# Expert stage: the 32 remainder slots of each expert transposed as a full 128-partition tile, and their down projection in four column groups

## The chip, the core and the metric

One core of a Trainium2 chip runs the whole program in one launch. The metric is the device time of one execution in microseconds, the median of several runs. The core has a matrix engine (TensorE, PE in the profile; its weight loads stand as PEld), VectorE (DVE), ScalarE (ACT), GpSimd (POOL) and SyncE (SP), which only issues transfers here. Data lie in SBUF, 128 partitions wide; TensorE writes to PSUM, eight banks of 512 float32 values per partition. All data are float32.

## The reference

One inference step of a one-layer encoder for 1024 prompt tokens and 32 sample tokens: a token mixer (sparse attention, gated linear attention and an mLSTM, with a shared input and output projection), a layer norm, and then a mixture of experts, which the change is about:

```python
gate = jnp.einsum('nk,nke->ne', wsel, jax.nn.one_hot(eidx, N_EXPERTS, dtype=F32))
out = jnp.zeros((B * T, D), F32)
for e in range(N_EXPERTS):
    h = jax.nn.silu(xf @ w_gate[e]) * (xf @ w_up[e])
    out = out + gate[:, e:e + 1] * (h @ w_down[e]).astype(F32)
```

There are 16 experts; each token goes to two. D is 1024 and the hidden width 256, so `w_gate[e]` and `w_up[e]` are 1024x256 and `w_down[e]` is 256x1024.

## The kernel before

The program has three stages. The **trunk** computes the mixer tile by tile (nine tiles of up to 128 tokens), the norm and the routing, and writes the normed rows and, for each expert, a list of the tokens that chose it. The **expert stage** (`mlps`) runs the 16 experts one after the other, each over 160 slots (`CAP`): 128 in block 0 and 32 more (`CB`), the remainder, in block 1. `combine` then gathers the two expert rows of each token and does the last norm.

In the expert stage every engine runs its own loop, and semaphores tie them together; each loop holds four experts (`NW`), with buffers by number.

- SyncE loads the three weights of an expert (1 MB each) three experts ahead into one of four sets `wg`, `wu`, `wd`; a set comes free when the down products of its expert are done (`ob_ps`).
- GpSimd loads the slot numbers `ids` and gathers the rows into `xg` (two buffers; block 1 fills partitions 0 to 31 only). A gather waits until the transposes of the expert two before are done. Behind its loop it loads the residual rows `xr` and the gains, and scales nine tiles.
- TensorE, in `body`: 64 instructions for gate and up into `GU` (32 float32 products, each of which runs as two instructions), then `turn` of the next expert, then the down products. `turn` transposes eight 128-column pieces of both blocks into the two halves `T[0]`, `T[1]` of a PSUM pair in turn, two pieces at a time. Down adds up two halves `f` of the hidden width, for block 0 into `OA` (128 rows) and for the remainder into `OB` (32 rows), 512 columns a product.
- ScalarE applies SiLU (`gate`), copies each filled half of `T` to `xgT` (four copies an expert; TensorE may use a half again once its copy is done, `xgT_copied`), copies `OA` to `rows` and issues the stores.
- VectorE multiplies gate and up to `hT` and copies `OB`.

A product of 128 contraction rows whose output has 32 rows uses 32 of TensorE's 128 columns; the profile writes its shape as 128*32. A full one is 128*128, and a transpose of 32 partitions is 32*128. Where the output of a product begins (partition 0, 32, 64 or 96) sets which 32 columns it uses: its column group. In the trunk, line 1397 has products of 64 output rows that begin at partition 0 and 64 in turn:

```python
for h in range(H):
    b = 64 * (h % 2)
    last = mmul(RA[b:b + 64, DV * (h // 2):DV * (h // 2) + DV], qk[0:n, 1, h, :], zvt[:, DV * h:DV * h + DV],
                start=True, stop=True)
```

There are four heads, so four products or eight instructions in a row, all of 96 columns. Line 1142 is the trunk's helper for transposes, line 1666 the gate and up products, 1655 and 1656 the transposes of the two blocks, 1677 the down products.

Of the kernel before, what the change touches and what calls it, by code (L numbers as in the profile page):

```python
# [22 lines left out]
D = 1024  # L23
# [1455 lines left out]
def mlps(nc, a, win, ident, ones, chosen_sum, expert, before, gatew, at_i, more_i, w_at, w_more, xr, g2, b2, ps, x1_d, slot_d, eo_d, em_d):  # L1479
    ctx = ExitStack()  # L1480
    S = semaphores(nc, ctx)
    with ctx:
# [9 lines left out]
        xgT = sb("xgT", [128, 2, KD, CAP])  # L1492
        gate = sb("gate", [128, 2, CAP])
        hT = sb("hT", [128, 2, CAP])
        rows = [sb(f"rows{j}", [128, 2, D]) for j in range(2)]
        most = sb("most", [128, NE])
        in_cap = sb("in_cap", [128, NT, 2])
        pos_f = sb("pos_f", [128, NT, 2])
# [21 lines left out]
        with nc.Block() as block:  # L1520
# [16 lines left out]
            @block.gpsimd  # L1537
            def _(pool):
                pool.sem_inc(S("xgT_ps"), 8)
                with pool.Fori(0, NE // NW) as i:  # L1540
                    for j in range(NW):
                        e = i * NW + j
                        with nc.allow_non_contiguous_dma("slot ids"):
                            pool.dma_start(ids[:, j, 0:1], slots_e[0:128, bass.ds(e, 1), 0]).then_inc(S(f"ids_loaded{j}"), 16)
                            pool.dma_start(ids[0:CB, j, 1:2], slots_e[128:CAP, bass.ds(e, 1), 0]).then_inc(S(f"ids_loaded{j}"), 16)
                        pool.wait_ge(S(f"ids_loaded{j}"), i * 32 + 32)
                        pool.sem_inc(S("pool_passed"), 1)
                        pool.wait_ge(S("xgT_ps"), e * 4 + 4)
                        pool.sem_inc(S("pool_passed"), 1)
                        for b, nb in ((0, 128), (1, CB)):  # L1550
                            pool.indirect_dma_start(  # L1551
                                out=xg[j % 2][0:nb, b, :], out_offset=None, in_=x1_d,
                                in_offset=bass.IndirectOffsetOnAxis(ap=ids[0:nb, j, b:b + 1], axis=0)).then_inc(S(f"xg_loaded{j % 2}"), 16)

                pool.dma_start(xr[:, 0:NPT, :], x1_d[0:SEQ].rearrange("(t p) d -> p t d", p=128)).then_inc(S("xr_loaded"), 16)
                pool.dma_start(xr[0:SMP, NPT, :], x1_d[SEQ:TOKENS]).then_inc(S("xr_loaded"), 16)
                pool.dma_start(g2[:], a["ln2_g"][0].partition_broadcast(128)).then_inc(S("xr_loaded"), 16)
                pool.dma_start(b2[:], a["ln2_b"][0].partition_broadcast(128)).then_inc(S("xr_loaded"), 16)
                pool.wait_ge(S("xr_loaded"), 64)
                for t in range(NT):  # L1560
                    x = xr[0:tokens(t), t, :]
                    nc.gpsimd.tensor_scalar(x, x, ALPHA, None, ALU.mult)

            @block.scalar
            def _(act):
# [6 lines left out]
                def turned(e, j):  # L1572

                    for u in range(4):
                        act.wait_ge(S("xgT_ps"), e * 4 + (u + 9))
                        A.activation(xgT[:, j % 2, 2 * u:2 * u + 2, :], T[u % 2][:, 0:2 * CAP].rearrange("p (k n) -> p k n", k=2),
                                     ACT.Copy).then_inc(S("xgT_copied"), 1)

                def body(i, j, e, last):
# [9 lines left out]
                    act.wait_ge(S("oa_copied"), e + 2)  # L1589
                    act.dma_start(rows_e[0:128, bass.ds(e, 1), :].rearrange("s one d -> s (one d)"), rows[j % 2][:, 0, :]).then_inc(S(f"rows_stored{j % 2}"), 16)  # L1590
                    act.wait_ge(S("ob_copied"), e + 2)
                    act.dma_start(rows_e[128:CAP, bass.ds(e, 1), :].rearrange("s one d -> s (one d)"), rows[j % 2][0:CB, 1, :]).then_inc(S(f"rows_stored{j % 2}"), 16)

                turned(0, 0)

# [7 lines left out]
            def _(dve):  # L1603
# [27 lines left out]
                with dve.Fori(0, NE // NW) as i:  # L1631
                    for j in range(NW):
# [5 lines left out]
                            V.tensor_tensor(hT[:, f, :], gate[:, f, :], GU[f][:, CAP:2 * CAP], ALU.mult).then_inc(S("h_ready"), 1)  # L1638
                        dve.wait_ge(S("ob_ps"), e + (NW + 1))
                        dve.wait_ge(S(f"rows_stored{j % 2}"), i * (16 * NW) + 32 * (j // 2 + 1))  # L1640
                        V.tensor_copy(rows[j % 2][0:CB, 1, :], OB[0:CB, :]).then_inc(S("ob_copied"), 1)  # L1641

            @block.tensor
            def _(pe):
# [4 lines left out]
                def turn(e, j, loaded):  # L1649
                    pe.wait_ge(S(f"xg_loaded{j % 2}"), loaded)  # L1650
                    for u in range(4):
                        pe.wait_ge(S("xgT_copied"), e * 4 + (u + 1))
                        for k in (2 * u, 2 * u + 1):
                            c = CAP * (k % 2)
                            E.transpose(T[u % 2][:, c:c + 128], xg[j % 2][:, 0, 128 * k:128 * k + 128], ident[:])
                            last = E.transpose(T[u % 2][:, c + 128:c + CAP], xg[j % 2][0:CB, 1, 128 * k:128 * k + 128], ident[0:CB, 0:CB])  # L1656
                        last.then_inc(S("xgT_ps"), 1)

                def body(i, j, e, last_one):
# [10 lines left out]
                        turn(e + 1, j + 1, i * (16 * NW) + 32 * ((j + 1) // 2 + 1))  # L1670
                    for f in range(2):
                        pe.wait_ge(S("h_ready"), e * 2 + (f + 3))
                        for out, c0, nb, sem in ((OA, 0, 128, "oa"), (OB, 128, CB, "ob")):
                            if f == 0:
                                pe.wait_ge(S(sem + "_copied"), e + 1)
                            for c in range(2):
                                last = E.matmul(out[0:nb, 512 * c:512 * c + 512], hT[:, f, c0:c0 + nb], wd[j][:, f, 512 * c:512 * c + 512],  # L1677
                                                start=(f == 0), stop=(f == 1))
                            if f == 1:
                                last.then_inc(S(sem + "_ps"), 1)  # L1680

                turn(0, 0, 32)
                each_expert(pe, body)
# [243 lines left out]
```

## Time and profile before

| what | us |
|---|---|
| median of three runs | 1513.97 (1511.3 to 1522.41) |
| span of the profiled execution, first to last instruction | 1520.2 |
| expert stage, first transpose to last product | 1108.8 to 1439.6 of the span |
| TensorE busy in the span | 1318.4 (87%) |
| mean granted TensorE clock over the span | 0.880 of 2.4 GHz |

The span lies within the range of the runs; the program's own time is about the span, a few us of start and end around it. All times of the rows are counted from the start of the span. A row of the order of time gives its start, how long it lasted, the engine, the line and the tiles (output, then inputs) with shapes, and in brackets how long its engine stood idle before it. Durations of single products overlap, since they are pipelined: the distance of two starts is what one costs. The granted clock is 1.00 at 2.4 GHz and 0.50 at 1.2 GHz.

### The profile page before, as it was taken

Reading aid. Unit: us, or ns where it says so; the run is one execution under the profiler, and the core shown is the slowest. Engines: PE = TensorE matmul, PEld = TensorE weight load, DVE = VectorE, ACT = ScalarE, POOL = GpSimd, SP = SyncE. Lnnn points to the kernel's source line nnn. Section 1 sums busy time; section 2 is a strip of 40 time slices with the busy share of each in tenths; the row PEclk is TensorE's granted clock in tenths of the full one; section 3 lists DMA queues with packets and bytes.
Section 4 is the critical chain, followed back from the end, with each engine's and each line's share of the span. In section 5 each row is a group of like instructions: output and inputs, shape, how many; then the busy total and the mean of one; then the engine's idle time right before and its main releaser. Section 6 shows DMA issues by size and latency. Waiting matters only on the chain. (4 is left out here: it accounts for less than half of the span.)

```text
span 1520.2 us, 16147 instructions
## 1 busy us (share of the span) xinstructions
PE 1318.4 (87%) x5597; PEld 813.6 (54%) x5597; DVE 775.7 (51%) x1787; ACT 398.4 (26%) x805; POOL 431.7 (28%) x460
## 2 busy tenths in 40 slices
PE   5898899999999999999898997996289999999800
PEld 2566565755656656656654544653156666666500
DVE  0024125778778878988897988333300000000078
ACT  1142424324324224224314212311011111111111
POOL 5103024052151251261055012002231111113487
PEclk9999899999999898999898988575679999999955
DMA  8966645536543443443333333001078766667163
GB/s 272 313 200 210 231 145 179 173 108 201 155 159 123 146 147 112 146 147 108 113 113 122 110 94 118 1 14 29 4 252 301 235 218 234 211 203 250 35 221 121
DMA packets 146265, 238.60 MB, mean 157 GB/s; under 512 B 17211, under 2 KB 117474, under 8 KB 146194
## 3 DMA queue, kind: packets, MB, share of 16 engines
q1 hardware_dynamic: 131298, 197.66, 40.3%
q0 software_dynamic: 10064, 29.16, 5.9%
q10 hardware_dynamic: 4832, 10.88, 2.3%
q8 instruction: 39, 0.64, 0.2%
q14 instruction: 32, 0.26, 0.1%
HBM read 211.38 MB, written 26.29 MB: 156 GB/s over the span
## 5 line engine op out<-in xcount | busy, mean ns | idle before, releaser
L1188 PE MATMUL bank_pair<-win,xT 128*128 128x384 f32 (+7 forms) x1152 | 450.6, 542 | 14.8 <-DMA win<-in_w_in 13.7
L1188 PEld LDWEIGHTS bank_pair<-win,xT 128*128 128x128 f32 (+1 forms) x1152 | 213.3, 193 | 192.0 <-issue 100.9
L897 DVE MAX8 top<-score 128x8 f32<-128x384 f32 (+6 forms) x201 | 174.9, 870 | 4.0
L898 DVE MATCH_REPLACE8 score<-top,score 128x384 f32<-128x384 f32 (+6 forms) x201 | 171.9, 855 | 0.0
L1282 PE MATMUL bank_pair<-w_out,yT 128*128 128x512 f32 (+1 forms) x288 | 131.2, 610 | 0.4 <-ACT yT L623 0.4
L1641 DVE COPY rows<-bank_pair 32x1024 f32<-32x1024 f32 x16 | 19.4, 1212 | 170.3 <-PE bank_pair L1677 170.3
L567 POOL TENSOR_TENSOR small<-small,pexp 128x4 f32<-128x4 f32 (+1 forms) x9 | 9.4, 1049 | 335.9 <-DVE small L1078 335.9
L1677 PE MATMUL bank_pair<-wd,hT 128*128 128x512 f32 (+1 forms) x192 | 98.8, 653 | 0.0
L1551 POOL DMA_INDIRECT xg<-x_rows,ids x32 | 30.1, 941 | 229.1 <-PE bank_pair L1656 215.9
L1282 PEld LDWEIGHTS bank_pair<-w_out,yT 128*128 128x128 f32 (+1 forms) x288 | 52.8, 186 | 74.0 <-issue 72.2
L1142 PE MATMUL bank_pair<-ident,lm 128*128 128x128 f32 (+2 forms) x234 | 43.2, 312 | 45.8 <-ACT lm L733 15.8
L1638 DVE TENSOR_TENSOR hT<-gate,bank_pair 128x160 f32<-128x160 f32 x32 | 10.3, 321 | 138.6 <-ACT gate L1583 138.6
L918 DVE CUSTOM_DVE_ANT_0 lm<-bank_pair,score 128x128 f32<-128x128 f32 (+8 forms) x36 | 26.0, 723 | 72.9 <-PE bank_pair L1225 50.4
L1142 PEld LDWEIGHTS bank_pair<-ident,lm 128*128 128x128 f32 (+2 forms) x234 | 31.8, 172 | 58.3 <-issue 33.2
L733 ACT ACTIVATE lm<-lm,small 128x128 f32<-128x128 f32 (+8 forms) x36 | 26.9, 748 | 132.0 <-DVE small L920 131.9
L1677 PEld LDWEIGHTS bank_pair<-wd,hT 128*128 128x128 f32 (+1 forms) x192 | 27.0, 160 | 61.5 <-issue 61.0
L1666 PEld LDWEIGHTS bank_pair<-xgT,wg 128*128 128x128 f32 x384 | 53.1, 190 | 10.1 <-issue 10.1
L1666 PE MATMUL bank_pair<-xgT,wg 128*128 128x160 f32 x384 | 57.3, 302 | 0.0
L598 POOL TENSOR_SCALAR rel<-rel,zw 128x512 f32<-128x512 f32 (+4 forms) x33 | 45.2, 1369 | 40.7 <-ACT rel L702 38.6
L1666 PE MATMUL bank_pair<-xgT,wu 128*128 128x160 f32 x384 | 56.1, 299 | 0.0
L1251 PEld LDWEIGHTS bank_pair<-va,pT 128*128 128x128 f32 (+1 forms) x296 | 45.4, 220 | 17.3 <-issue 11.7
L1666 PEld LDWEIGHTS bank_pair<-xgT,wu 128*128 128x128 f32 x384 | 53.5, 190 | 0.0
(339 smaller groups left out, 2091.7 us busy)
## 6 DMA issues: line engine op xcount, KB each, us to landing
win<-in_w_in SPq DMA_DIRECT2D x90, 768.0 KB, 4.4
win<-in_w_in SPq DMA_DIRECT2D x18, 1024.0 KB, 5.3
win<-in_w_in SPq DMA_DIRECT2D x18, 840.0 KB, 5.2
win<-in_w_in SPq DMA_DIRECT2D x18, 800.0 KB, 4.6
wg<-in_w_exp_gate SPq DMA_DIRECT2D x12, 1024.0 KB, 6.2
wu<-in_w_exp_up SPq DMA_DIRECT2D x12, 1024.0 KB, 9.4
wd<-in_w_exp_down SPq DMA_DIRECT2D x12, 1024.0 KB, 11.1
expert_rows<-rows ACTq DMA_DIRECT2D x16, 512.0 KB, 3.3
```

The lines of the kernel that those rows point to most:

```text
L598: ins = G.tensor_scalar(r if h else sc, r, zw[0:n, t % 2, h:h + 1], None, ALU.mult)
L733: A.activation(lm[0:n, 0:K], lm[0:n, 0:K], ACT.Exp, bias=sm(n, ANEG + h), scale=HA ** -0.5, accum_out=sm(n, ASUM + h)).then_inc(S("probs_r ...
L897: step(V.max(top8[0:n], sc))
L898: step(V.match_replace(sc, top8[0:n], sc, NEG))
L918: step(V.tensor_tensor_reduce(lm[0:n, 0:K], SC[0:n, 0:K], score[0:n, t % 2, 0:K], 1.0, -3.0e38, ALU.add, ALU.max, sm(n, AMAX + h)))
L1142: tr = lambda out, in_: E.transpose(out, in_, ident[0:in_.shape[0], 0:in_.shape[0]])
L1188: last = mmul(zb[0:n, 0:w], xT[:, kk, 0:n], win[:, i % NWIN, k, 0:w], start=(kk == 0), stop=(kk == KD - 1))
L1251: last = mmul(MA[0:n, HA * h:HA * h + HA], pT[0:kb, g % 2, b - b0, 0:n], vv[:, HA * h:HA * h + HA], start=(b == 0), stop=(128 * b + kb == K))
L1282: last = mmul(SC[0:n, 512 * c:512 * c + 512], yT[:, k, 0:n], w_out[:, k, 512 * c:512 * c + 512], start=(k == 0), stop=(k == KD - 1))
L1551: pool.indirect_dma_start(out=xg[j % 2][0:nb, b, :], out_offset=None, in_=x1_d, in_offset=bass.IndirectOffsetOnAxis(ap=ids[0:nb, j, b:b + ...
L1666: last = E.matmul(GU[f][:, CAP * m:CAP * m + CAP], w[:, k, 128 * f:128 * f + 128], xgT[:, j % 2, k, :], start=(k == 0), stop=(k == KD - 1))
L1677: last = E.matmul(out[0:nb, 512 * c:512 * c + 512], hT[:, f, c0:c0 + nb], wd[j][:, f, 512 * c:512 * c + 512], start=(f == 0), stop=(f == 1))
```

## The change

The remainder is treated in a new shape in two places, and its result lies in another form.

- **Transposes.** Block 1 is transposed over all 128 partitions, like block 0, so all 16 transposes of an expert have one shape. Partitions 32 to 127 of block 1, which no gather writes, are cleared once by GpSimd before its loop, in both `xg` buffers. A half of `T` now holds four pieces of 128 columns; ScalarE copies the first 160 of each 256.
- **Down products.** Block 0 comes first as a whole, both halves `f`. Then the remainder: eight products of 256 columns, four for each `f`, whose outputs go to partitions 0, 32, 64 and 96 of the same 256 columns of `OB`: quarter `q` of the model width into column group `q`. `OB` is then 128 partitions by 256.
- **Copy and store.** VectorE copies 128x256 into a new tile `rest`; ScalarE stores it with a pattern that puts the quarters back in place.

```diff
-        rows = [sb(f"rows{j}", [128, 2, D]) for j in range(2)]
+        rows = [sb(f"rows{j}", [128, 1, D]) for j in range(2)]
+        rest = [sb(f"rest{j}", [128, D // 4]) for j in range(2)]
...
                 pool.sem_inc(S("xgT_ps"), 8)
+                for x in xg:
+                    nc.gpsimd.memset(x[:, 1, :], 0.0).then_inc(S("rest_cleared"), 1)
+                pool.wait_ge(S("rest_cleared"), 2)
                 with pool.Fori(0, NE // NW) as i:
...
-                        A.activation(xgT[:, j % 2, 2 * u:2 * u + 2, :], T[u % 2][:, 0:2 * CAP].rearrange("p (k n) -> p k n", k=2),
+                        A.activation(xgT[:, j % 2, 2 * u:2 * u + 2, :], T[u % 2].rearrange("p (k n) -> p k n", k=2)[:, :, 0:CAP],
                                      ACT.Copy).then_inc(S("xgT_copied"), 1)
...
-                    act.dma_start(rows_e[128:CAP, bass.ds(e, 1), :].rearrange("s one d -> s (one d)"), rows[j % 2][0:CB, 1, :]).then_inc(S(f"rows_stored{j % 2}"), 16)
+                    act.dma_start(rows_e[128:CAP, bass.ds(e, 1), :].rearrange("s one (q d) -> q s (one d)", q=4), rest[j % 2][:]).then_inc(S(f"rows_stored{j % 2}"), 16)
...
-                        V.tensor_copy(rows[j % 2][0:CB, 1, :], OB[0:CB, :]).then_inc(S("ob_copied"), 1)
+                        V.tensor_copy(rest[j % 2][:], OB[:, 0:256]).then_inc(S("ob_copied"), 1)
...
                         for k in (2 * u, 2 * u + 1):
-                            c = CAP * (k % 2)
-                            E.transpose(T[u % 2][:, c:c + 128], xg[j % 2][:, 0, 128 * k:128 * k + 128], ident[:])
-                            last = E.transpose(T[u % 2][:, c + 128:c + CAP], xg[j % 2][0:CB, 1, 128 * k:128 * k + 128], ident[0:CB, 0:CB])
+                            for b in range(2):
+                                c = 256 * (k % 2) + 128 * b
+                                last = E.transpose(T[u % 2][:, c:c + 128], xg[j % 2][:, b, 128 * k:128 * k + 128], ident[:])
                         last.then_inc(S("xgT_ps"), 1)
...
                         pe.wait_ge(S("h_ready"), e * 2 + (f + 3))
-                        for out, c0, nb, sem in ((OA, 0, 128, "oa"), (OB, 128, CB, "ob")):
-                            if f == 0:
-                                pe.wait_ge(S(sem + "_copied"), e + 1)
-                            for c in range(2):
-                                last = E.matmul(out[0:nb, 512 * c:512 * c + 512], hT[:, f, c0:c0 + nb], wd[j][:, f, 512 * c:512 * c + 512],
-                                                start=(f == 0), stop=(f == 1))
-                            if f == 1:
-                                last.then_inc(S(sem + "_ps"), 1)
+                        if f == 0:
+                            pe.wait_ge(S("oa_copied"), e + 1)
+                        for c in range(2):
+                            last = E.matmul(OA[:, 512 * c:512 * c + 512], hT[:, f, 0:128], wd[j][:, f, 512 * c:512 * c + 512],
+                                            start=(f == 0), stop=(f == 1))
+                    last.then_inc(S("oa_ps"), 1)
+                    pe.wait_ge(S("ob_copied"), e + 1)
+                    for f in range(2):
+                        for q in range(4):
+                            last = E.matmul(OB[CB * q:CB * q + CB, 0:256], hT[:, f, 128:CAP], wd[j][:, f, 256 * q:256 * q + 256],
+                                            start=(f == 0), stop=(f == 1))
+                    last.then_inc(S("ob_ps"), 1)
```

How TensorE's instructions stand, from the first quarter of the transposes of one expert to the down products of the one before it. The rows give the line, the operation, output and inputs, and the output's shape; one down product stands for two instructions on the chip. Before, the end of the transposes and the down products:

```order
L1652 REGISTER_ALU
L1655 MATMUL bank_pair<-ident,xg 128x128
L1656 MATMUL bank_pair<-ident,xg 128x32
L1655 MATMUL bank_pair<-ident,xg 128x128
L1656 MATMUL bank_pair<-ident,xg 128x32
L1672 REGISTER_ALU
L1677 MATMUL bank_pair<-win,hT 128x512 x2
L1677 MATMUL bank_pair<-win,hT 32x512 x2
L1672 REGISTER_ALU
L1677 MATMUL bank_pair<-win,hT 128x512 x2
L1677 MATMUL bank_pair<-win,hT 32x512 x2
```

And after, the same place:

```order
L1656 REGISTER_ALU
L1660 MATMUL bank_pair<-ident,xg 128x128 x4
L1676 REGISTER_ALU
L1680 MATMUL bank_pair<-win,hT 128x512 x2
L1676 REGISTER_ALU
L1680 MATMUL bank_pair<-win,hT 128x512 x2
L1686 MATMUL bank_pair<-win,hT 32x256 x8
```

The two shapes of transpose no longer take turns, and the 32-row products stand in one run of eight behind all of the 128-row ones.

On GpSimd, where the expert stage begins, before:

```order
L1537 UNCONDITIONAL_BRANCH
L1540 UNCONDITIONAL_BRANCH
L1540 ISA
L1544 DMA ids<-slot_tokens 128x1
L1545 ISA
L1545 DMA ids<-slot_tokens 32x1
```

And after:

```order
L1538 UNCONDITIONAL_BRANCH
L1542 MEMSET xg 128x1024 x2
L1544 UNCONDITIONAL_BRANCH
L1544 ISA
L1548 DMA ids<-slot_tokens 128x1
L1549 ISA
L1549 DMA ids<-slot_tokens 32x1
```

Two clears now stand ahead of the first load of slot numbers, and of every gather behind it.

## Rows read from the trace of the kernel before

**Rows 1.** The page, busy time, share of the span and instructions of TensorE

```profile
PE 1318.4 (87%) x5597; PEld 813.6 (54%) x5597; DVE 775.7 (51%) x1787; ACT 398.4 (26%) x805; POOL 431.7 (28%) x460
```

**Rows 2.** Windows: start:end, us, busy us by engine (instructions), granted clock, DMA share, GB/s

```profile
1108.80:1439.60 330.80, 330.05 (x1536) 212.19 (x1536) 28.54 (x48) 57.89 (x115) 71.44 (x71) 0.95 0.65 219
...
1165.00:1185.00 20.00, 20.00 (x89) 12.18 (x88) 1.85 (x3) 3.38 (x7) 3.01 (x4) 0.91 0.63 209
1185.00:1205.00 20.00, 20.00 (x101) 13.21 (x100) 1.85 (x3) 4.66 (x8) 3.04 (x4) 1.00 0.69 233
```

**Rows 3.** Groups by form, expert stage: busy us, mean ns of one, idle before

```profile
L1677 PE MATMUL bank_pair<-wd,hT 128*32 128x512 f32 x96 | 45.9, 600 | 0.0
```

**Rows 4.** Order of time, TensorE, three experts: their gate and up products

```profile
1198.21 8.96 PE L1666 MATMUL bank_pair<-xgT,win 128*128 128x160 f32 x64
...
1219.50 2.44 PE L1666 MATMUL bank_pair<-xgT,wg 128*128 128x160 f32 x16
...
1239.20 0.40 PE L1666 MATMUL bank_pair<-xgT,wg 128*128 128x160 f32 x1
```

**Rows 5.** Order of time, TensorE, transposes of one expert, then its down products

```profile
1228.30 0.27 PE L1655 MATMUL bank_pair<-ident,xg 128*128 128x128 f32 x1
1228.50 0.24 PE L1656 MATMUL bank_pair<-ident,xg 32*128 32x32 f32 x1
1228.67 0.33 PE L1655 MATMUL bank_pair<-ident,xg 128*128 128x128 f32 x1
...
1229.11 0.33 PE L1655 MATMUL bank_pair<-ident,xg 128*128 128x128 f32 x1
...
1231.70 0.70 PE L1677 MATMUL bank_pair<-wd,hT 128*128 128x512 f32 x1
```

**Rows 6.** Order of time, TensorE in the trunk: eight full transposes

```profile
628.31 1.04 PE L1142 MATMUL bank_pair<-ident,y 128*128 128x128 f32 x8
```

**Rows 7.** Order of time, first expert: last copy of the transposes, then products

```profile
1114.07 0.44 ACT L1576 ACTIVATE xgT<-bank_pair 128x320 f32<-128x320 f32 x1 [0.86 <-PE bank_pair L1656]
...
1114.64 10.51 PE L1666 MATMUL bank_pair<-xgT,win 128*128 128x160 f32 x64 [0.61 <-ACT xgT L1576]
```

**Rows 8.** Order of time, weight loads of down products in the expert of rows 5

```profile
1234.50 0.11 PEld L1677 LDWEIGHTS bank_pair<-wd,hT 128*32 128x32 f32 x1 [0.32 <-issue]
1235.45 0.30 PEld L1677 LDWEIGHTS bank_pair<-wd,hT 128*128 128x128 f32 x2 [0.84 <-issue]
1235.99 0.19 PEld L1677 LDWEIGHTS bank_pair<-wd,hT 128*128 128x128 f32 x1 [0.24 <-issue]
1236.42 0.19 PEld L1677 LDWEIGHTS bank_pair<-wd,hT 128*128 128x128 f32 x1 [0.24 <-issue]
```

**Rows 9.** Order of time, line 1397: all of it, and what had begun by 616.98

```profile
616.97 0.55 PE L1397 MATMUL bank_pair<-zv,qk 128*64 128x96 f32 x8
...
616.97 0.30 PE L1397 MATMUL bank_pair<-zv,qk 128*64 128x96 f32 x2
```

**Rows 10.** Windows: a stretch of transposes, what followed it, and one in the trunk

```profile
1206.60:1210.01 3.41, 3.41 (x20) 2.21 (x18) 0.32 (x1) 1.53 (x4) 0.00 (x0) 1.00 0.83 320
1210.01:1213.42 3.41, 3.41 (x7) 1.51 (x6) 0.00 (x0) 0.52 (x2) 1.62 (x2) 0.50 0.15 17
936.90:1008.60 71.70, 61.68 (x255) 43.22 (x256) 28.86 (x110) 25.03 (x50) 7.30 (x12) 0.50 0.08 26
```

**Rows 11.** Order of time, GpSimd: the largest clear in the trunk

```profile
17.80 0.73 POOL L488 MEMSET zm<- 128x776 f32 x1
```

**Rows 12.** Order of time, VectorE in the expert of rows 5

```profile
1219.71 1.21 DVE L1641 COPY rows<-bank_pair 32x1024 f32<-32x1024 f32 x1 [11.77 <-PE bank_pair L1677]
...
1228.91 0.32 DVE L1638 TENSOR_TENSOR hT<-gate,bank_pair 128x160 f32<-128x160 f32 x1 [4.02 <-ACT gate L1583]
```

**Rows 13.** Order of time, GpSimd behind its last gather

```profile
1375.51 1.00 POOL L1551 DMA_INDIRECT xg<-x_rows,ids  x1 [18.07 <-PE bank_pair L1656]
...
1398.08 24.67 POOL L1562 TENSOR_SCALAR xr<-xr 128x1024 f32<-128x1024 f32 x9 [17.77 <-DMA b<-in_ln_b]
```

## The prediction

> **What bounds the kernel now.** I read the page's engine totals first, then the expert stage by windows, its groups by form, and its order of time. On the page TensorE is busy for 87% of the span and no other engine for more than 51% [rows 1]. In the expert stage (330.8 us from the first transpose to the last product) it is busy for 330.05 us, with a mean granted clock of 0.95 and the DMA engines at a share of 0.65 [rows 2]. What TensorE is spared here therefore comes off the span, as long as nothing else becomes late. The groups by form show that the down products that make only 32 output rows are as many as those that make 128 and last 0.60 us each [rows 3]. The order of time gives one expert: gate and up start at 1219.50, transposes at 1228.30, down products at 1231.70, the next expert at 1239.20, so 8.80 + 3.40 + 7.50 = 19.70 us [rows 4, 5].
>
> **Transposes.** Now a 128-partition transpose is followed by a 32-partition one; a pair takes 0.43 us (1228.67 to 1229.11), eight pairs 3.40 us [rows 5]. Yet eight full transposes in a row take 1.04 us, the last itself 0.27, so 0.11 us from one to the next [rows 6]: the changes of shape cost, not the columns. Sixteen full ones need 15 x 0.11 + 0.11 = 1.75 us if nothing waits. But ScalarE empties two buffers in turn, at 0.44 us a copy [rows 7], and a quarter of the work is now four transposes, 0.44 us too. Step by step: the fourth transpose ends at 0.60, the first copy at 1.07; TensorE follows a copy 0.13 us later (copy end 1114.51, product start 1114.64 [rows 7]), so the third quarter starts at 1.20. The second copy ends at 1.53, the last quarter runs from 1.66 to 2.10. I take 2.1 us, a saving of 1.3 an expert, 19.7 us for 15. The bounds are 1.75 us (no wait, 25 saved) and today's 3.40 (nothing). The first expert's transposes run at half clock, 5.8 us from 1108.8 to 1114.64 [rows 2, 7]; at twice 0.11 us each, with the closing copy, some 4.3: 1.5 us saved.
>
> **Down products.** A float32 product is two instructions. The weight loads tell the steps at 512 columns: 0.43 us (1235.99 to 1236.42), alike in both shapes. From 1234.50 to 1235.45 are two steps and the return from 32 to 128 columns, 0.09 us for the change; the next step, to 1235.99, is 0.54, so 0.11 more [rows 8]. An expert has four changes, 7.50 - 16 x 0.43 = 0.6 us in all, 0.15 each. After it there are two, and the 128-row part is eight steps, 3.43 us. The remainder becomes 16 instructions of 256 columns, 0.21 us each. What they take hangs on whether four groups of 32 columns run at once. The trace has two groups of 64 at once: the products of line 1397 alternate between output partitions 0 and 64, and their eight instructions of 96 columns are over in 0.55 us, one lasts up to 0.30, and two have begun within the first 0.02 us [rows 9]. Four pairs then begin (0.55 - 0.30) / 3 = 0.08 us apart, which is what 96 columns cost one alone (0.43 x 96 / 512). Today's 32-row products all lie in one column group, and their two halves follow each other at 0.43 us; so the two that start together belong to different heads. I take full overlap: four steps of 0.21 and 0.2 us for what of the changes falls to this part, 1.06. Down is then 4.5 us and saves 3.0, 48 us over 16 experts. With no overlap it is 3.43 + 0.2 + 3.43 = 7.06 us, a saving of 0.44, or 7. The other end is worse still: if each of the eight changes of group also cost 0.2 us, the dearest change of shape here, down would take 8.66 us and lose 1.16 an expert, 19 in all. The nearest row is that of line 1397, with the same data type and column groups in turn.
>
> The Trainium skill, page "TensorE: Matmul & The Clock Gate", section "Part 3: Packing small matmuls", says that matmuls start and end strictly in program order; by that rule the first of the rivals below would hold, 17 us above the forecast. The two starts of line 1397 [rows 9] disagree with it. The same section's measured gain of 2.38 times with three column groups agrees with overlap as such, and no run here shows three or four.
>
> **The clock.** It falls to 0.50 right behind a stretch of transposes: 1.00 from 1206.60 to 1210.01, which are nearly all transposes, then 0.50 until 1213.42 [rows 10]. That expert took 1219.50 - 1198.21 = 21.29 us, 1.59 more than its neighbour [rows 4]. The windows of 20 us from 1125 to 1405 show seven such dips (one in the second of [rows 2], 0.91 against 1.00), together 11.1 us. All seven follow some 3.4 us of transposes; eight stretches of the same length are followed by none. After the change a stretch has 2.1, so I count the dips as gone (the bounds: 0 and 11.1; if they stay, 1450). The Trainium skill, same page, section "Part 4: PE-mode transpose", says that transposes do not count as busy for the clock in the way that products do. The dips agree; by that rule any stretch of transposes is a risk, and sixteen full ones still make one.
>
> **Start, end and queues.** GpSimd clears two 128x1024 tiles and waits for that before it loads the first slot numbers; the first gather is queued behind it, and TensorE waits for the gather. A clear of 776 columns took 0.73 us [rows 11]; so 2 x 0.97 and a wait, 2.0 us lost. The last copy, 32x1024 in 1.21 us [rows 12], becomes 128x256; a VectorE operation on 160 columns of PSUM took 0.32 [rows 12], so about 0.4: 0.8 saved. The remainder's store goes to 128 partitions of 1 KB; ScalarE's queue has room and the buffer is used again two experts later, so nothing. The wait for the remainder's last copy now stands behind the 128-row products, and that copy is done more than 10 us before [rows 8, 12]. The wait for the second half of the hidden rows moves ahead of two products: those rows are ready at 1229.23, 2.5 us before the products begin [rows 4, 12], and after the change still over 1 us before.
>
> **Who is late next.** Weights, gathers and stores: the DMA share is 0.69 in undisturbed windows of 20 us [rows 2], so 13.6 us of work an expert against the coming 15.4. That is 0.88, and loads run three experts ahead: hidden, with 1.8 us to spare. GpSimd: from the last gather at 1375.51 it loads the residual rows (waits 17.8 us) and scales nine tiles until 1422.75 [rows 13], 47.2 us. TensorE has left at that point the down products of expert 12, two whole experts and one without transposes: 4.5 + 2 x 15.4 + 8.8 + 4.5 = 48.6, less 0.9 that had passed since the transposes. GpSimd stays hidden by 0.5 us and the last copy and store behind TensorE; a slower load would soon show.
>
> **Sum.** 19.7 + 1.5 + 48 + 11.1 + 0.8 - 2.0 = 79 us. Against the profiled execution (span 1520.2; the slowest run, 1522.41, is 2.2 above it) this gives 1443; against the median of 1513.97 it gives 1435. The quicker runs may already lack some dips, so I take 1439.
>
> **The rivals.** *Overlap in program order:* in the program the two halves of a product stand side by side; if starts keep that order, only the second half of one group's product overlaps the first half of the next group's. That is nine steps of 0.21 us in place of four, 1.07 us an expert, 17 us: 1456. For it speaks that all other products here do run in order. *The groups don't overlap:* the change would not do what it says; 2.56 us an expert, 41 us: 1480, and with a price at each change of group (1.6 us more) 1506. *The end or the DMA takes over:* the scaling by GpSimd ends last, or weights come late, 3 to 10 us: about 1445. *The clock stays down, and the kernel gets slower:* a busy engine alone does not hold it, since from 936.9 to 1008.6 TensorE was busy for 61.68 of 71.70 us at 0.50 [rows 10], with small shapes and transposes. The stage after has 4.3 + 10.4 + 15 x 10.9 + 16 x 4.5 = 250 us of TensorE's work; the gain of 79 us is used up when the mean granted clock of the stage falls to 250 / 329 = 0.76, and below that the time is over 1518, for instance 1540. Against it: 12.2 of 15.4 us are the same full-array products that hold 1.00 now.
>
> **How the numbers follow.** Forecast 0.60; program order 0.15; no overlap 0.10; end or DMA 0.10; clock 0.03; the rest anything. The range from 1423 to 1463 takes in the forecast, the lost clock dips, the end and the program-order case, and leaves out no overlap and the clock. A measurement of this kernel tells about 1% from no change; all cases but the clock's lie more than 1% (15 us) below 1514, some ends of the second and third excepted: faster 0.95, same 0.02, slower 0.03.
>
> **What would show it.** In the profile after: 16 transposes 0.11 us apart with two short waits for ScalarE; the remainder's 16 instructions over in about 1.1 us, four begun almost at once; an expert of 15.4 us; no dip in the clock between 1130 and the stage's end; two clears of about 1 us ahead of the first slot numbers. I am wrong if the remainder takes 1.9 us or more, if GpSimd or a weight load releases TensorE, or if the dips stay.

## The result, and the profile after

The changed kernel took 1444.08 us (median of four runs, 1429.1 to 1448.7), the kernel before, on the same chip, 1517.43 (four runs): a ratio of 0.951, 95% interval 0.944 to 0.9585. It is faster by 73 us. The forecast was 1439. Timed once more later (e10 below) it took 1441.12 against 1518.40, 77 us less.

The profiled execution is the quickest of the four, 1429.1 us with a span of 1427.3. On the page TensorE is as busy by share as before [rows 1], with less work:

```profile
PE 1226.1 (86%) x5725; PEld 791.4 (55%) x5725; DVE 760.8 (53%) x1787; ACT 398.6 (28%) x805; POOL 433.6 (30%) x462
```

The windows of the stage, in the columns of [rows 2]: the whole stage, a window near its start, the two windows of [rows 2], and the window of [rows 10] in which the clock had been down.

```profile
1096.80:1346.00 249.20, 246.54 (x1664) 197.59 (x1664) 16.66 (x47) 58.01 (x115) 70.96 (x71) 0.99 0.85 290
1105.00:1125.00 20.00, 19.33 (x136) 16.23 (x135) 1.39 (x4) 4.97 (x9) 5.42 (x8) 1.00 1.06 357
1165.00:1185.00 20.00, 19.91 (x140) 16.87 (x139) 1.39 (x4) 4.97 (x9) 3.03 (x4) 1.00 1.03 343
1185.00:1205.00 20.00, 19.82 (x141) 16.53 (x140) 1.39 (x4) 4.89 (x11) 3.03 (x4) 1.00 1.01 344
...
1210.01:1213.42 3.41, 3.41 (x27) 3.41 (x27) 0.09 (x1) 0.00 (x0) 0.00 (x0) 1.00 0.66 228
```

The stage is 249.1 us long (1096.85 to 1345.93) where it was 330.7. Its clock is 1.00 behind the first transposes, and no window shows a dip. The DMA share is 0.85 on average, but 1.01 to 1.06 in the three windows up to 1205, where before it was 0.63 and 0.69. The share adds up the times of the packets, and these can overlap, so it can pass 1. The order of time of TensorE in one expert and of ScalarE beside it, the answer to [rows 4, 5, 7]:

```profile
1209.45 2.44 PE L1670 MATMUL bank_pair<-xgT,wg 128*128 128x160 f32 x16
...
1218.24 2.22 PE L1660 MATMUL bank_pair<-ident,xg 128*128 128x128 f32 x16
1220.30 3.60 PE L1680 MATMUL bank_pair<-wd,hT 128*128 128x512 f32 x8
1223.83 1.07 PE L1686 MATMUL bank_pair<-wd,hT 128*32 128x256 f32 x16
1224.83 3.39 PE L1670 MATMUL bank_pair<-xgT,win 128*128 128x160 f32 x23
```

```profile
1218.88 0.88 ACT L1580 ACTIVATE xgT<-bank_pair 128x320 f32<-128x320 f32 x2
1220.06 0.88 ACT L1580 ACTIVATE xgT<-bank_pair 128x320 f32<-128x320 f32 x2 [0.31 <-PE bank_pair L1660]
```

Start to start, an expert is 8.79 of gate and up, 2.06 of transposes, 3.53 of 128-row products and 1.00 of the remainder: 15.38 us, where it was 19.70. How the remainder begins shows in two windows of the same view: up to 0.07 us behind its first start (first row) four instructions have begun, up to 0.37 us (second row) eight.

```profile
1223.83 0.42 PE L1686 MATMUL bank_pair<-wd,hT 128*32 128x256 f32 x4
1223.83 0.64 PE L1686 MATMUL bank_pair<-wd,hT 128*32 128x256 f32 x8
```

The waits of TensorE in the stage (us in total, times, longest):

```profile
PE bank_pair L1660 <- issue: 11.0, 1, 11.0
PE bank_pair L1670 <- ACT xgT L1580: 0.6, 1, 0.6
PE bank_pair L1670 <- DMA wd<-in_w_exp_down: 0.6, 1, 0.6
```

The first lies ahead of the stage, the second is that of [rows 7]. The third is new: the second expert waits 0.6 us for its weights. GpSimd ahead of the first gather, the answer to [rows 11]:

```profile
1085.32 1.84 POOL L1542 MEMSET xg<- 128x1024 f32 x2 [6.22 <-POOLq L104]
1088.30 0.60 POOL L1548 DMA_DIRECT2D ids<-slot_tokens  x1 [1.14 <-issue]
...
1091.81 1.02 POOL L1555 DMA_INDIRECT xg<-x_rows,ids  x1 [2.33 <-issue]
```

The same in the kernel before:

```profile
1099.87 0.60 POOL L1544 DMA_DIRECT2D ids<-slot_tokens  x1 [6.98 <-POOLq L104]
...
1103.68 1.02 POOL L1551 DMA_INDIRECT xg<-x_rows,ids  x1 [2.32 <-issue]
```

From the end of the trunk's last GpSimd work to the first gather it is now 6.22 + 6.49 = 12.71 us; before it was 6.98 + 3.81 = 10.79. The clears cost 1.9 us.

The end has got longer. From the last product to the first gather of the combine stage it is 9.63 us (1345.93 to 1355.56), before 6.68 (1439.47 to 1446.16). The last products and the first gathers, after and then before:

```profile
1344.86 1.07 PE L1686 MATMUL bank_pair<-wd,hT 128*32 128x256 f32 x16
...
1355.56 1.05 POOL L1843 DMA_INDIRECT r<-expert_rows,at_i  x1 [8.85 <-PEq L1812]
```

```profile
1432.01 7.46 PE L1677 MATMUL bank_pair<-wd,hT 128*128 128x512 f32 x16
...
1446.16 1.04 POOL L1835 DMA_INDIRECT r<-expert_rows,at_i  x1 [23.40 <-PEq L1804]
```

GpSimd's scaling [rows 13] and the last store on ScalarE's queue, in order of time, and then by line 1521, the end of the block, at which all engines meet (duration in ns, first and last start; the end of an engine's DRAIN row is taken as its arrival):

```profile
1322.02 24.69 POOL L1566 TENSOR_SCALAR xr<-xr 128x1024 f32<-128x1024 f32 x9 [19.01 <-DMA b<-in_ln_b]
```

```profile
1346.46 0.55 ACTq L1596 DMA_DIRECT2D expert_rows<-rest  x1
```

```profile
L1521 POOLq EVENT_SEMAPHORE  x2: 17/17/17, 1352.4 to 1352.5; - x2
L1521 POOLq DRAIN  x1: 30365/30365/30365, 1322.0 to 1322.0; - x1
...
L1521 ACTq DRAIN  x1: 8/8/8, 1351.5 to 1351.5; - x1
```

And the kernel before, where this is line 1520:

```profile
L1520 POOLq DRAIN  x1: 30345/30345/30345, 1398.0 to 1398.0; - x1
...
L1520 ACTq DRAIN  x1: 8/8/8, 1442.9 to 1442.9; - x1
```

Two things are seen. ScalarE, which waits for the last store, arrives at 1351.5, 5.6 us after the last product (before: 1442.9, 3.5 us). And GpSimd's drain, which begins with the scaling, lasts 30.37 us, until 1352.3, which is 5.6 us behind the end of the scaling's row (1346.71); so GpSimd is the last to arrive, by 0.8 us. In the kernel before the drain of 30.35 us lasts until 1428.4, long before the last product. What GpSimd does in these 5.6 us the rows don't show. They aren't the price of longer scalings: the drain ends 5.63 us behind the last row in all twelve profiled executions, with nine scalings and, in e8 and e9 below, with seven.

What the store does shows in the busy share of the DMA engines in 40 equal slices of 1346.8 to 1351.4:

```profile
DMA  6999979699973520206010032222222221000000
```

The 512 KB of the 128-row store fill all 16 engines for 1.4 us. The remainder's 128 KB go on until 1351.0; for the last 1.4 us the share is 0.2, about three to four engines of 16. In the kernel before, from 1439.3 to 1442.8, the remainder's store is the second block, 0.6 us long:

```profile
DMA  0009899997979997970000000099669510000000
```

The same two views also count the packets, after first and then before; the third row is e7's (below, 1367.3 to 1371.0), in which the remainder is stored as four:

```profile
DMA packets 276, 0.66 MB, mean 142 GB/s; under 512 B 20, under 2 KB 148, under 8 KB 276
DMA packets 192, 0.66 MB, mean 187 GB/s; under 512 B 32, under 2 KB 32, under 8 KB 192
DMA packets 336, 0.66 MB, mean 177 GB/s; under 512 B 80, under 2 KB 208, under 8 KB 336
```

Those under 512 B are packets of 4 bytes, which carry none of the rows. With two stores in the kernel before there are 32, with five in e7 80, so 16 for a store that uses all engines. In the kernel after there are 20: 16 for the 128-row store and 4 for the remainder's. That agrees with four engines, by a count and not by a share.

Accounting, profiled against profiled: the stage -81.6 us, its start +1.9, its end +2.9, together -76.8. The medians differ by 73 and 77. The rest of the 93 us between the two spans isn't the change's: the unchanged trunk ended 14 us earlier in this execution, and the combine stage took 71.7 us for 74.0 (73.4 when profiled again in e10).

### The profile page after: what moved, and what is told of

Same layout as the page of the kernel before. It is cut to its first block and busy times, and to the rows that moved or that the text cites. A ratio compares the mean times of both kernels' runs of the same rounds, so it can differ in the third digit from the quotient of the medians.

```text
span 1427.3 us, 16405 instructions
## 1 busy us (share of the span) xinstructions
PE 1226.1 (86%) x5725; PEld 791.4 (55%) x5725; DVE 760.8 (53%) x1787; ACT 398.6 (28%) x805; POOL 433.6 (30%) x462
## 5 line engine op out<-in xcount | busy, mean ns | idle before, releaser
L1645 DVE COPY rest<-bank_pair 128x256 f32<-128x256 f32 x16 | 6.8, 425 | 91.6 <-PE bank_pair L1686 91.6
L530 POOL DMA_INDIRECT slot_tokens<-tok_id,slots_i x18 | 18.5, 1029 | 115.0 <-DVE chosen_sum L997 95.0
L1251 PE MATMUL bank_pair<-va,pT 128*128 128x64 f32 (+1 forms) x296 | 47.5, 304 | 0.4 <-ACT pT L623 0.4
```

The lines of the kernel that those rows point to most:

```text
L1251: last = mmul(MA[0:n, HA * h:HA * h + HA], pT[0:kb, g % 2, b - b0, 0:n], vv[:, HA * h:HA * h + HA], start=(b == 0), stop=(128 * b + kb == K))
```

## The experiments

The theory on record: the remainder's gain comes from four column groups at work at the same time; that of the transposes from full shapes in a row, which also takes the clock's dips away. Rivals: groups overlap only as far as program order lets them; the gain comes from something else in the rewrite (the shorter copy, the order of the products); the dips come from the 32-row products or from the length of a stretch of transposes. The measured numbers below are the stage from first transpose to last product, and the parts of an expert start to start.

**e1 and e2: each part alone.** e1 has the transposes, their copies and the clears of the changed kernel, and the down products, the remainder's copy and the stores of the one before; e2 the reverse. Excerpts, against the kernel after:

```
# e1
-  E.matmul(OB[CB * q:CB * q + CB, 0:256], hT[:, f, 128:CAP], wd[j][:, f, 256 * q:256 * q + 256], ...)
+  E.matmul(out[0:nb, 512 * c:512 * c + 512], hT[:, f, c0:c0 + nb], wd[j][:, f, 512 * c:512 * c + 512], ...)
# e2
-  last = E.transpose(T[u % 2][:, c:c + 128], xg[j % 2][:, b, 128 * k:128 * k + 128], ident[:])
+  E.transpose(T[u % 2][:, c:c + 128], xg[j % 2][:, 0, 128 * k:128 * k + 128], ident[:])
+  last = E.transpose(T[u % 2][:, c + 128:c + CAP], xg[j % 2][0:CB, 1, 128 * k:128 * k + 128], ident[0:CB, 0:CB])
```

> Full transposes and the clears as in the changed kernel, down products, copy and store as before. If the changes of shape are what transposes cost and long stretches of transposes are what drops the clock: transposes 2.06 us an expert, down 7.40, an expert 18.26 us, no dip in the clock, TensorE's stage from the first transpose to the last product 294 us (before 330.6, changed 249.1), time 33 to 36 us below the kernel before, and 6.7 us from the last product to the first gather of the next stage, as before. Rival, the 32-row products are what drops the clock: about seven dips stay, stage 305 us.

> Four column groups with the new copy and store, transposes in the old two shapes, no clears. First theory: transposes 3.4 us, down 4.6, an expert 16.85 us, dips of the clock behind about half of the stretches of transposes, stage 273 us and 1.6 us more for each dip, time 42 to 52 us below the kernel before; 9.6 us from the last product to the first gather, because the store of 128 pieces of 1 KB lands late. Rival on the clock (32-row products one after the other drop it): no dip. Rival on the end (GpSimd's scaling holds it up): 6.7 us there, since this stage is longer and GpSimd done long before.

e1: 1480.81 us against 1517.88, ratio 0.974 (0.967 to 0.980). Stage 296.4 us, transposes 2.06, down 7.39, no dip, end 6.68. e2: 1464.39, ratio 0.9665 (0.962 to 0.971). Stage 278.2, transposes 3.41, down 4.6, and the end at 8.82, although GpSimd's drain was over 4.6 us before ScalarE arrived: so the longer end begins with the store. Of the dips of the clock three were left, behind stretches of 3.41 us with alternating shapes; one of them by its window:

```profile
1234.40:1237.80 3.40, 3.40 (x6) 1.69 (x6) 0.00 (x0) 0.44 (x1) 1.88 (x2) 0.50 0.25 58
```

What follows: both parts work alone, and the products of 32 rows don't bring the dips, since e1 has them all and no dip.

**e3 and e4: group by group, and one group.** e3 writes the remainder's products in another order, all of one group and then all of the next; e4 keeps e3's order and its 16 instructions of 256 columns, but puts all their results into column group 0, with the copy and the store of the kernel before. Excerpts:

```
# e3, against after
-  for f in range(2):
-      for q in range(4):
+  for q in range(4):
+      for f in range(2):
# e4, against e3
-  E.matmul(OB[CB * q:CB * q + CB, 0:256], ...)
+  E.matmul(OB[0:CB, 256 * q:256 * q + 256], ...)
```

> As the changed kernel, but the remainder's products in the order of the groups, both halves of the hidden width of a group next to each other, so four instructions of one group follow each other in the program. If each column group takes its own instructions in turn, whatever stands between them: the remainder 1.0 us, as in the changed kernel, stage 249 us. If starts keep the program's order: only a group's last step overlaps the next one's first, 13 steps, 2.7 us, stage 276 us.

> As the changed kernel, with the same eight products of 256 columns for the remainder, group by group, but all into output partitions 0 to 31, so in one column group; copy and store as before. If the gain is overlap between groups: 16 steps of 0.21 us, the remainder 3.6 us, an expert 18.0, stage 291 us. If the gain came from fewer changes of shape and from the order alone: the remainder stays near 1 us, stage 250 us.

One run each. e3: 1440.86 us (before 1517.88), stage 249.3, remainder 1.02. e4: 1473.58, stage 289.5, remainder 3.57. The 16 instructions of one expert, e3 first:

```profile
1218.96 1.09 PE L1686 MATMUL bank_pair<-wd,hT 128*32 128x256 f32 x16
```

```profile
1230.16 3.64 PE L1685 MATMUL bank_pair<-wd,hT 128*32 128x256 f32 x16
```

In e3 four instructions have again begun within 0.08 us of the first, and eight within 0.33 (first two rows); in e4 one has begun within 0.09 us (third row).

```profile
1234.37 0.44 PE L1686 MATMUL bank_pair<-wd,hT 128*32 128x256 f32 x4
1234.37 0.66 PE L1686 MATMUL bank_pair<-wd,hT 128*32 128x256 f32 x8
```

```profile
1230.16 0.40 PE L1685 MATMUL bank_pair<-wd,hT 128*32 128x256 f32 x1
```

What follows: the same instructions cost 3.57 us in one group and 1.02 in four (1.00 in the kernel after), so the gain is overlap. And it doesn't hang on the order in the program: in e3 the first four instructions written all go to group 0, which in e4 takes one each 0.22 us. Four that begin within 0.08 us must then belong to four groups, so that later instructions of other groups overtake earlier ones. The records don't name the group; this is read from the total and from the spacing, and the spacing bears it out: the four starts lie 7 ns apart in the kernel after and 13 ns in e3, twice as much, and the first instructions of two groups lie two apart in the one program and four in the other.

**e5 and e6: what the shapes cost, and what lowers the clock.** e5 is the kernel before with the four transposes of a quarter in the order 128, 128, 32, 32 partitions; e6 is the kernel after with all transposes of a quarter done twice. Excerpts:

```
# e5, against before
+  for k in (2 * u, 2 * u + 1):
       E.transpose(T[u % 2][:, c:c + 128], xg[j % 2][:, 0, ...], ident[:])
+  for k in (2 * u, 2 * u + 1):
       last = E.transpose(T[u % 2][:, c + 128:c + CAP], xg[j % 2][0:CB, 1, ...], ident[0:CB, 0:CB])
# e6, against after
-  for k in (2 * u, 2 * u + 1):
+  for k in (2 * u, 2 * u + 1) * 2:
```

> The kernel before, with the four transposes of a quarter in the order 128, 128, 32, 32 partitions instead of 128, 32, 128, 32. Theory (each change of shape costs TensorE about 0.1 us, the work of a 32-partition transpose no more than that of a full one): eight changes fewer in each expert, 3.40 us of transposes become about 2.6, the stage 330.7 - 15 x 0.8 = 319 us or less. Rival (a 32-partition transpose itself takes 0.3 us): the transposes stay at 3.4 us, whatever the order. On the clock: if a stretch of transposes as long as 3.4 us lets it drop, the seven dips go with the shorter stretch; if the 32-partition form does, they stay.

> The kernel after, with every full transpose done twice, so that a stretch of transposes is as long as before the change without having a 32-partition one: 32 x 0.109 = 3.5 us for 2.06, the period 15.39 + 1.4 = 16.8 us, the stage 249 + 15 x 1.4 = 270 us. Theory (the length of the stretch between matmuls lets the clock drop): dips come back in a part of the experts, 3 to 8 of 15. Rival (the small form or its gaps do it): none. ScalarE's copies are faster than the doubled quarters, so that TensorE should wait for none of them.

One run each. e5: 1491.9 us (before 1521.68), transposes 2.37 for 3.41, stage 302.9, no dip. e6: 1462.14 us, transposes 3.49, stage 271.8, no dip. A quarter of e5, and the clock of both stages behind their first transposes (e5's window first):

```profile
1236.61 0.44 PE L1655 MATMUL bank_pair<-ident,xg 128*128 128x128 f32 x2
1236.97 0.31 PE L1658 MATMUL bank_pair<-ident,xg 32*128 32x32 f32 x2
1237.21 0.44 PE L1655 MATMUL bank_pair<-ident,xg 128*128 128x128 f32 x2
```

```profile
1120.00:1410.00 290.00, 290.00 (x1485) 191.92 (x1484) 28.47 (x47) 55.52 (x111) 65.48 (x63) 1.00 0.72 243
```

```profile
1110.00:1375.00 265.00, 264.39 (x1882) 221.52 (x1881) 16.67 (x47) 56.11 (x112) 68.74 (x68) 1.00 0.79 272
```

What follows: eight changes of shape fewer save 1.04 us, 0.13 each on average, with the same work; the rival that a small transpose is itself dear falls. Start to start in e5, a small one behind a small one takes 0.084 us, less than the 0.109 of a full one in e9 below; a step into the other shape takes 0.20 or 0.15. So the kernel before could have had 28 us of its stage by a change of order alone (15.6 us of transposes, the rest mainly the dips). On the clock the theory that a stretch of transposes need only be long gets no support: in one execution each, 3.49 us of full ones in e6 lowered it in none of 15 experts, 3.41 us of alternating ones in seven (before) and in three (e2). What decides in which of them is open.

**e7: the remainder's store as four.** The store has the four groups as its outermost dimension. e7 issues one store for each group instead (an excerpt, against the kernel after).

```
-  act.dma_start(rows_e[128:CAP, ...].rearrange("s one (q d) -> q s (one d)", q=4), rest[j % 2][:])
+  for q in range(4):
+      act.dma_start(rows_e[128:CAP, ..., 256 * q:256 * q + 256], rest[j % 2][CB * q:CB * q + CB, :])
```

> The kernel after, with the remainder's store issued as four stores of 32 partitions instead of one whose outermost dimension is the four groups. Theory (one store with an outermost dimension of four is spread over four DMA engines only, 32 pieces of 1 KB one behind the other on each): the last store has landed about 3.5 us after TensorE's last product, against 5.4 us; the combine stage starts hardly earlier, since GpSimd, whose scaling then arrives last, holds it at 8.4 to 9.6 us after the last product. Rival (128 pieces of 1 KB take that long however they are spread): 5.3 us as now. If the four loaded engines also delay the weights, the wait of 0.6 us at expert 1 gets shorter.

e7 took 1452.64 us in its one run (before 1521.68). ScalarE arrived 4.1 us after the last product (1370.5 against 1366.45) where it had been 5.6, though the four issues alone took 2.15 us. But the first gather came 10.93 us after it, later than in the kernel after, since GpSimd arrived at 1374.2:

```profile
L1521 POOLq DRAIN  x1: 30348/30348/30348, 1343.8 to 1343.8; - x1
...
L1521 ACTq DRAIN  x1: 8/8/8, 1370.5 to 1370.5; - x1
```

The store part of the theory holds; the expected 8.4 to 9.6 us was too low, GpSimd arriving 3.6 us behind ScalarE here and not 0.8. The second expert's wait for weights was longer (2.3 us), so the four loaded engines aren't what it comes from.

**e8, e9 and e10: what can be mended.** e8 takes e7's stores, clears the tiles on VectorE, lets VectorE scale the last two of the nine tiles, and has VectorE copy the odd quarters of the transposes. e9 is e8 with all copies on ScalarE again, but a third buffer for the transposes: the remainder now fills only one of the two banks that it used to, and the other is free. e10 is the kernel after, unchanged, timed beside e9.

```
# e9, excerpts against after (stores as in e7)
-  nc.gpsimd.memset(x[:, 1, :], 0.0)
+  V.memset(x[:, 1, :], 0.0)
-  T = [ps[1][:, 0:512], ps[1][:, 512:1024]]
+  T = [ps[1][:, 0:512], ps[1][:, 512:1024], ps[3][:, 512:1024]]
-  pe.wait_ge(S("xgT_copied"), e * 4 + (u + 1))
+  if u in (0, 3):
+      pe.wait_ge(S("xgT_copied"), e * 4 + (2 if u == 0 else 3))
-  for t in range(NT):
+  for t in range(NT - 2):
+  for t in range(NT - 2, NT):
+      V.tensor_scalar(x, x, ALPHA, None, ALU.mult)
```

> The kernel after with four things mended: the two clears on VectorE instead of GpSimd, the remainder's store as four stores, the last two tiles of the end's scaling on VectorE, and the copies of the odd quarters of transposes on VectorE, those of the even ones on ScalarE. Expected: the stage's start 2 us earlier, 2.06 -> 1.75 us of transposes (15 x 0.31 = 4.6 us), 9.6 -> 6.8 us between the last product and the first gather of the combine stage; in all 9 us less than after, 1435 us, a ratio of 0.945 to before. Rival (the weights are the bound of the first experts, and the DMA engines are busy 0.85 of the stage): the transposes' gain turns into waits for weights, and the time is 1439 us.

> The kernel after with the two clears on VectorE, the remainder's store as four stores, the last two tiles of the end's scaling on VectorE, and a third buffer for the transposes in the half of the fourth bank pair that the remainder's products no longer use; ScalarE makes all copies. In the two-engine variant the transposes stayed at 2.11 us, since both engines' copies begin only 0.3 us after a quarter's last transpose and so the third quarter still waited for its buffer. Theory (the wait is for the buffer): 16 x 0.109 = 1.75 us of transposes for 2.06, no wait among them; with the start 2.5 us earlier and 2.6 us less at the end some 9 us less than after. Rival (the copies themselves are the bound, and the down products then wait): transposes 2.06 us or the same sum with the next phase.

> The kernel after, unchanged, timed on the same chip as the variant with the third buffer. Expected: 0.952 of before as in its first runs (0.944 to 0.9585), some 9 us over the variant. If the weights' arrival at the second expert depends on when the trunk ends, its wait differs from the 0.6 us of the first profile, between nothing and 2.4 us.

e8: 1435.76 us, ratio 0.944 (0.940 to 0.948). Its end came out as expected (7.05 us), its transposes did not: 2.11 us, since the first copy ends no earlier than before, so that the third quarter waits as it did, and VectorE's copy (0.49 us to ScalarE's 0.44) then holds the fourth by another 0.06 us. e9: 1430.74 us, ratio 0.942 (0.937 to 0.947), against 0.950 (0.946 to 0.9545) of e10, 1441.12 us. It is 10.4 us less than the kernel after on the same chip, where 9 had been expected; the intervals touch, but five of e9's six runs are quicker than the quickest of e10's. The profile shows where it comes from: in e9 the transposes are done in 1.75 us without a wait, and GpSimd is no longer the last to arrive.

```profile
1229.47 1.91 PE L1667 MATMUL bank_pair<-ident,xg 128*128 128x128 f32 x16
1231.22 3.60 PE L1687 MATMUL bank_pair<-wd,hT 128*128 128x512 f32 x8
```

```profile
L1521 POOLq DRAIN  x1: 24885/24885/24885, 1332.1 to 1332.1; - x1
...
L1521 ACTq DRAIN  x1: 8/8/8, 1358.7 to 1358.7; - x1
```

Its end is 7.27 us (e10: 10.12), its stage 246.2 (e10: 249.7), and the clears no longer stand ahead of the first gather (10.80 us behind the trunk's last GpSimd work, against 12.72 in e10). So this is the quickest of the versions here, 5.8% below the kernel before. The second expert's data came late in both: in e9 TensorE waited 2.43 us for it ahead of the transposes, in e10 for its weights behind them:

```profile
1124.12 2.44 PE L1670 MATMUL bank_pair<-xgT,wg 128*128 128x160 f32 x16 [1.24 <-DMA wd<-in_w_exp_down]
```

## Why the prediction was right

The forecast of 1439 us lies 5 us under the first median and 2 under the second. The sum of 79 us stands against 76.8 by the profiles; that the forecast was put in the middle between 1443 and 1435, since quicker runs may lack some dips, no run bears out or refutes. Its mechanism, overlap of four groups and full shapes in a row, is the one the runs show. By its terms:

- *Transposes, 3.40 to 2.1, 19.7 us.* Measured 3.41 to 2.06 in all 15, 20.2 us. One wait for ScalarE, not two: the first copy ends at 1.07 us as reckoned, TensorE follows it 0.05 us later and not 0.13, and the second copy ends at 1.51, so the fourth quarter's buffer is free by the time the third is through. The bound of 1.75 is what e9 reaches with a third buffer.
- *First expert, 5.8 to 4.3.* Measured 5.82 to 4.26.
- *Down, 7.50 to 4.5, 48 us.* Measured 7.50 to 4.53, 47.4 us. The 128-row part takes 3.53 and the remainder 1.00, where 3.43 and 1.06 stood; probably one change of shape lies in the other part.
- *Clock, 11.1 us.* Summing what the seven dips added to the parts of their experts gives 11.4 us, and all are gone. The reason was half right: that they follow 3.4 us of transposes is true of every one, but in e6 the length alone did nothing. The risk that the prediction still saw in sixteen full ones showed in none of the 15 stretches of the kernel after.
- *Last copy, 0.8.* 1.21 to 0.42. But the store behind it took up more than this (below).
- *Clears, -2.0.* Measured -1.9, given back in e9.
- *DMA share 0.88.* Measured 0.85 over the stage, so the weights stay hidden on the whole; but the share is about 1 until about 1205, and the second expert waits 0.6 us (1.2 and 2.3 in other executions). By the prediction's own mark, "if GpSimd or a weight load releases TensorE", it was wrong here, and again at the end (below); in the stage this is partly set off, since the kernel before lost 1.55 us in its first expert, between gate and up and the next transposes, and this one nothing. Such a wait for the second expert's data stood in every execution but two, sometimes before its transposes and sometimes behind; what decides its length was not settled. That these 1.55 us went was no term of the sum, and nor were the costs below: in part the total came out by luck.

Two steps failed, both at the end, and together they cost 2.9 us, 2.1 and 0.8. The first is "ScalarE's queue has room and the buffer is used again two experts later, so nothing": true for 15 experts, but nothing covers the last store, and it landed 2.1 us later behind the last product, although its copy was 0.8 us shorter. The trace shows a share of 0.2 while most of it runs and four of the 4-byte packets for 16, and e7 takes 1.6 us of it back. The Trainium skill, page "DMA: Bandwidth & Descriptors", section "Why a DMA increments its semaphore by 16 and not by 1", states the rule: the number of engines is the largest one up to 16 that divides the slowest dimension of both access patterns. For a store with four groups outermost that is four; the share and the four packets agree, and the page would have told it before the run.

The second is "GpSimd stays hidden by 0.5 us and the last copy and store". It rested on the end of the scaling's row [rows 13], 1422.75. But the drain ended only at 1428.4, 5.6 us later, so the margin was not there. GpSimd arrives last by 0.8 us in the kernel after, 0.2 in e3, 1.4 in e10 and 3.6 in e7; in e2 and e6, where it is done before ScalarE, the end is still 8.8 us for 6.7, so 2.1 are the store's. GpSimd and the weights are the third rival's mechanism. In the kernel after they cost 0.8 + 0.6 = 1.4 us, less than its 3 to 10, on top of a gain that came as forecast; the store's 2.1 us stood in no rival. The medians lie between the two cases.

Of the other rivals, overlap in program order would have given a remainder of 2.1 us; it measured 1.00, and e3 shows that the order doesn't matter. The Trainium skill, page "TensorE: Matmul & The Clock Gate", section "Part 3: Packing small matmuls", says that matmuls start and end strictly in program order. For column groups, e3 is against it. No overlap is what e4 does, 3.57 us. The clock never came near its rival's point of decision, 0.76: the stage's mean was 0.99.

## What to carry over

When outputs have 32 rows, spreading them over the idle column groups made 16 instructions cost as much as four and a half in one group, in whatever order they were written; and instructions of different shapes belong in runs, not in turn. The last store and the engine that is just hidden decide the end of a stage: look at how many DMA engines a store's outermost dimension leaves it, and read when an engine arrives from its drain at the end of the block, not from the end of its last row. After a gain of this size look again at each buffer that a wait names and at what the change has set free: here the freed bank removed the wait.

## What had not been expected of the hardware

- Column groups take their instructions independently: four begin, each 7 ns behind the other (13 in e3), and the following four 0.2 us later, even where the program has them one group after the other.
- Four groups together need 1.00 us where one needs 3.57, 3.6 times less.
- A change between 128 and 32 partitions costs a transpose 0.13 us on average (before against e5), more than the 0.109 us of a full transpose itself (e9).
- GpSimd's drain ends 5.63 us behind the row of the last scaling, in twelve of twelve executions: 30.4 us for nine scalings whose rows add up to 24.7, 24.9 for seven whose rows add up to 19.2. Why, the rows don't show.
- How many DMA engines a store uses shows in its packets of 4 bytes: 16 for each store of the kernel before, 4 for the one with the four groups outermost.
